# Stick-breaking attention in units of both heads of a pair, 128 queries and at most 512 keys

## The chip, the cores and the metric

One core of one Trainium2 chip runs the kernel. The metric is the device time of one launch in microseconds (us). A time is the median of several runs; one further execution was profiled, and every row of a trace is from it.

## The reference, cut to what matters

One layer of a decoder trunk on 1024 tokens of width 1024, all float32. A projection feeds three groups of heads: RWKV-7 (6 heads of 64), an RG-LRU, and stick-breaking attention (6 heads of 64). Then follow an output projection, a LayerNorm, a top-2 mixture of 16 experts and a second LayerNorm. The attention of one head, for each block of 128 queries (`i` = 0 to 7), is:

```python
kv_len = q0 + SBA_BLOCK
z = jnp.einsum('bhtd,bhsd->bhts', q[:, :, q0:kv_len], k[:, :, :kv_len]) * scale
mask = s_idx < t_idx
log_keep = jnp.where(mask, jax.nn.log_sigmoid(-z), 0.0)
after = lax.cumsum(log_keep, axis=3, reverse=True) - log_keep
attn = jnp.where(mask, jnp.exp(jax.nn.log_sigmoid(z) + after), 0.0)
outs.append(jnp.einsum('bhts,bhsd->bhtd', attn, v[:, :, :kv_len]))
```

The cumulative sum runs from the last key to the first, over at most 1024 keys.

## The kernel before

**Stages.** Every engine has its own program, and semaphores order them. The stages are: projection with the RG-LRU and the preparation of RWKV; the loop over 12 batches (the stage of the change, 373 to 900 us); output projection, first norm and router (900 to 1078 us); the mixture of experts (to about 1540 us); the last norm.

**The loop over batches.** A batch `b` is the RWKV delta rule on 256 tokens of one pair of heads: `mats_pe`, `mats_act`, `mats_dve` and `mats_pool`. It begins with products and masks (L646, L765), transposes (L656, L660), and then inverts triangular matrices in 5 levels. Each level is a chain over three engines: TensorE makes 16 small products (L602), ScalarE copies them out of PSUM (L742), TensorE makes 32 more, and VectorE writes them under a mask, first `lower`, then `upper` (L762). After the levels come L683, L689 to L707 and four state steps (L719, L726, L797), each of the last three with 4 bf16 matmuls of `keep_clock` (L629), which keep TensorE at work while it waits. After every fourth batch `rnorm_*` normalizes a pair's output.

**The attention between them.** The generators `mats_*` yield at 16 places (`GAPS`) in a batch. At each, `side_by_side` puts one piece of the attention into each engine's program: step `j` of `sba_pe`, `sba_act` and `sba_dve`. So the order on each engine is fixed when the kernel is built. A unit of the attention is one head, one block of 128 queries and all its keys (128 to 1024), 48 units in all, four steps each:

- kind 0: TensorE makes the scores z in `PS[0]` (L917, the head's 64 rows of the array; one matmul for each 512 keys) and adds the causal mask (L919, bf16). ScalarE makes Exp of the unit before (L951), and then Abs, Exp and Ln of this one (L965, L967, L969).
- kinds 1 and 2: TensorE transposes the unit before, up to four tiles in a step (L932), VectorE copies them out (L989). In kind 1 VectorE also takes max(z, 0) (L997), and in kind 2 it scans the keys backwards (L977) and subtracts (L979).
- kind 3: TensorE sums attention times v over all key tiles of the unit before (L940, the head's 64 columns of the array).

A float32 matmul stands in the trace as two records, a float32 transpose as one. The blocks of a pair are taken in the order 0, 7, 1, 6, 2, 5, 3, 4, so that four units (16 steps) always hold nine tiles for each head.

**The mixture of experts.** A loop of 21 rounds with two experts side by side on the column halves (L1499): gate, up, eight transposes of the next round's rows (L1493), four of the hidden values in two groups (L1529, L1534) whose copies VectorE and ScalarE make (L1589, L1564), and the down products. Ahead of the loop `keep_clock` runs 10 bf16 matmuls while the first rows are gathered.

Of the kernel before, what the change touches and what calls it, by code (L numbers as in the profile page):

```python
# [22 lines left out]
P = 128  # L23
# [3 lines left out]
HD = 64  # L27
# [27 lines left out]
def layer_kernel(nc, t, out):  # L55
    ctx = ExitStack()
    with ctx:
# [21 lines left out]
        pc = sb("pc", [P, NPAIR, S // C])  # L79

# [66 lines left out]
        s_bz, s_bx, s_bv = sem("z_in_psum"), sem("attn_transposed"), sem("attn_v_in_psum")  # L147
        s_bd, s_ba, s_bt, s_bo = sem("attn_dve"), sem("attn_act"), sem("attnT_copied"), sem("attn_out_copied")
# [668 lines left out]

# [66 lines left out]
        NU = NPAIR * NT * 2  # L884
        Rl = TT[:, 0, :]

        def unit(u):
            g, n, hh = u // (2 * NT), (u // 2) % NT, u % 2
            i = n // 2 if n % 2 == 0 else NT - 1 - n // 2
            return g, i, hh, slice(hh * HD, (hh + 1) * HD), (i + 1) * P, 1 + (i > 0)  # L890

        def group(i, k):

            cut = (i + 2) // 2
            return (0, cut) if k == 0 else (cut, i + 1)

        def groups(u):

            return sum(unit(x)[5] for x in range(u))
        BD, BA = 3, 4  # L900


        def sba_pe(e, j):
            u, kind = j // 4, j % 4
            if kind == 0:
                if u >= NU:
                    return
                g, i, hh, h, kv, ng = unit(u)
                wait(e, s_pe, LRU_T + SBA_T + NT)
                wait(e, s_bd, BD * u)  # L910
                for pair in range(1, NPAIR - 1):
                    if j == norm_step(pair) + 1:
                        wait(e, s_na, 2 * (pair - 1) + 1)
# [11 lines left out]
            g, i, hh, h, kv, ng = unit(u)  # L925
            if kind <= ng:
                k = kind - 1
                wait(e, s_ba, BA * u + 4)
                wait(e, s_bt, groups(u) + k)
                lo, hi = group(i, k)  # L930
# [882 lines left out]
```

## Time and profile before

| | |
|---|---|
| median of 3 runs | 1605.48 us (1601.74 to 1607.9) |
| the profiled execution's own time | 1605.52 us |
| its span, first to last instruction | 1603.8 us |
| outside the span | 1.7 us |
| TensorE busy | 1422.8 us (89%) |
| VectorE busy | 597.4 us (37%) |
| ScalarE busy | 431.4 us (27%) |
| mean granted TensorE clock | 0.944 of 2.4 GHz |

PE is TensorE's matmuls, PEld its weight loads, DVE VectorE, ACT ScalarE, POOL GpSimd. The granted clock of TensorE is either 1.0 (2.4 GHz) or 0.5 (1.2 GHz); a mean over a stretch lies between. The busy share of PE includes the tail of each matmul, so it is no measure of how full the array is.

### The profile page before, as it was taken

Reading aid. Unit: us, or ns where it says so; the run is one execution under the profiler, and the core shown is the slowest. Engines: PE = TensorE matmul, PEld = TensorE weight load, DVE = VectorE, ACT = ScalarE, POOL = GpSimd, SP = SyncE. Lnnn points to the kernel's source line nnn. Section 1 sums busy time; section 2 is a strip of 40 time slices with the busy share of each in tenths; the row PEclk is TensorE's granted clock in tenths of the full one; section 3 lists DMA queues with packets and bytes.
Section 4 is the critical chain, followed back from the end, with each engine's and each line's share of the span. In section 5 each row is a group of like instructions: output and inputs, shape, how many; then the busy total and the mean of one; then the engine's idle time right before and its main releaser. Section 6 shows DMA issues by size and latency. Waiting matters only on the chain.

```text
span 1603.8 us, 22792 instructions
## 1 busy us (share of the span) xinstructions
PE 1422.8 (89%) x9346; PEld 763.4 (48%) x9346; DVE 597.4 (37%) x1010; ACT 431.4 (27%) x671; POOL 102.7 (6%) x177
## 2 busy tenths in 40 slices
PE   8999999998888788887888999839999999999980
PEld 3444444455666566655666455514444444444430
DVE  2143103444667566656666333361011101111017
ACT  1044123322444334443434311121111111111113
POOL 0000000001000000000000000000110111111110
PEclk9999999999999988997999999859999999999995
DMA  4110111000000000002000225068749949959415
GB/s 185 38 40 31 35 39 40 27 0 1 1 2 2 1 1 2 1 2 106 1 2 2 81 92 210 27 238 299 271 137 352 338 128 320 340 168 317 117 32 217
DMA packets 61012, 170.14 MB, mean 106 GB/s; under 512 B 3184, under 2 KB 3328, under 8 KB 60928
## 3 DMA queue, kind: packets, MB, share of 16 engines
q1 hardware_dynamic: 54384, 145.31, 24.4%
q0 software_dynamic: 6544, 23.62, 6.1%
q8 instruction: 63, 1.03, 0.3%
q14 instruction: 21, 0.17, 0.0%
HBM read 144.28 MB, written 24.64 MB: 105 GB/s over the span
## 4 chain that ended last, share of the span: by engine, by line
PE 74%; DVE 15%; ACT 4%; issue 4%; DMA 2%; SPq 0%; DVEq 0%; POOL 0%; POOLq 0%; ACTq 0%
PE PS L1499 27%; PE PS L193 16%; PE PS L1123 7%; PE PS L602 4%; PE PS L917 3%; DVE TT L977 3%; PE PS L202 3%; DVE XS L762 2%; PE PS L940 2%; DVE XS L765 2%; PE PS L1493 1%; PE PS L932 1%; PE PS L336 1%; DMA YT<-x1d,RK 1%; PE PS L683 1%
## 5 line engine op out<-in xcount | busy, mean ns | idle before, releaser
L1499 PE MATMUL PS<-RK,YT 128*64 128x512 f32 x736 | 323.6, 596 | 0.8 <-DVE YT L1589 0.8
L193 PE MATMUL PS<-XS 128*128 128x512 f32 x672 | 294.6, 598 | 7.1 <-DMA XS<-in_xT 6.9
L1499 PE MATMUL PS<-XS,YT 128*64 128x512 f32 x656 | 287.3, 595 | 6.4 <-DVE YT L1589 5.5
L193 PEld LDWEIGHTS PS<-XS 128*128 128x128 f32 x672 | 127.3, 191 | 172.6 <-issue 164.2
L1499 PEld LDWEIGHTS PS<-XS,YT 128*64 128x64 f32 x656 | 89.0, 138 | 171.8 <-issue 170.7
L602 PE MATMUL PS<-XS 64*64 64x64 f32 x2688 | 110.9, 231 | 36.3 <-DVE XS L762 24.7
L602 PEld LDWEIGHTS PS<-XS 64*64 64x64 f32 x2688 | 95.1, 143 | 54.6 <-DVE XS L762 39.1
L1585 DVE TENSOR_TENSOR YT<-YT,PS 128x256 f32<-128x256 f32 x42 | 15.8, 419 | 271.8 <-PE PS L1499 271.8
L1123 PE MATMUL PS<-RK,YT 128*128 128x512 f32 x256 | 111.1, 593 | 1.1 <-DVE YT L1026 1.1
L1499 PEld LDWEIGHTS PS<-RK,YT 128*64 128x64 f32 x736 | 99.8, 137 | 20.7 <-issue 20.7
L1499 PE MATMUL PS<-SQ,YT 128*64 128x512 f32 x424 | 104.0, 593 | 1.9 <-DVE YT L1589 1.9
L1123 PEld LDWEIGHTS PS<-RK,YT 128*128 128x128 f32 x256 | 48.1, 190 | 59.8 <-issue 57.9
L762 DVE COPY_PREDICATED XS<-lower,PS 128x512 f32<-128x512 uint8 x60 | 43.5, 726 | 80.6 <-PE PS L602 69.7
L1598 DVE TENSOR_SCALAR YT<-PS,RK 128x512 f32<-128x512 f32 x21 | 15.8, 751 | 142.6 <-PE PS L1499 142.6
L977 DVE TENSOR_TENSOR_SCAN TT<-XS,TT 128x128 f32<-128x128 f32 (+7 forms) x48 | 66.0, 1374 | 1.0 <-ACT XS L969 0.5
L917 PE MATMUL PS<-SQ 64*128 64x512 f32 (+3 forms) x144 | 65.1, 562 | 0.6 <-ACT TT L1014 0.6
L742 ACT COPY XS<-PS 128x512 f32<-128x512 f32 x60 | 35.1, 584 | 109.2 <-PE PS L602 108.3
L1499 PEld LDWEIGHTS PS<-SQ,YT 128*64 128x64 f32 x424 | 38.0, 137 | 49.7 <-issue 49.7
L940 PE MATMUL PS<-XS,SQ 128*64 128x128 f32 x432 | 59.8, 285 | 0.0
L762 DVE COPY_PREDICATED XS<-upper,PS 128x512 f32<-128x512 uint8 x60 | 43.2, 720 | 36.0 <-PE PS L602 35.4
L1488 POOL DMA_INDIRECT sums<-YT,RK x21 | 33.6, 1600 | 328.9 <-DVE YT L1598 328.9
L1499 PE MATMUL PS<-YT 128*64 128x512 f32 x120 | 53.6, 593 | 0.0
(361 smaller groups left out, 1760.7 us busy)
## 6 DMA issues: line engine op xcount, KB each, us to landing
XS<-in_w_in SPq DMA_DIRECT2D x21, 512.0 KB, 3.2
XS<-in_w_gate SPq DMA_DIRECT2D x5, 2048.0 KB, 12.3
XS<-in_w_upx SPq DMA_DIRECT2D x5, 2048.0 KB, 18.0
XS<-in_w_down SPq DMA_DIRECT2D x5, 2048.0 KB, 9.1
RK<-in_w_gate SPq DMA_DIRECT2D x5, 2048.0 KB, 20.2
RK<-in_w_upx SPq DMA_DIRECT2D x5, 2048.0 KB, 22.6
RK<-in_w_down SPq DMA_DIRECT2D x5, 2048.0 KB, 13.1
SQ<-in_w_gate SPq DMA_DIRECT2D x4, 2048.0 KB, 21.3
```

Of the source, the lines that this page charges most:

```text
L193: m = e.matmul(acc[:, half * HB:(half + 1) * HB], XS[:, 8 + n % 4, kt * P:(kt + 1) * P], XS[:, kt, half * HB:(half + 1) * HB], start=kt == ...
L202: m = e.matmul(acc[:, 0:SBA_W], XS[:, kt, i * P:(i + 1) * P], wv[:, kt, :], start=kt == 0, stop=kt == KT - 1)
L602: ins = e.matmul(acc[r, m * P + d * C:m * P + (d + 1) * C], left[r, m, r], right[r, m, r], start=True, stop=True)
L742: e.copy(M1[:, :, :], four(RB(3))).then_inc(s_ma, 1)
L762: return e.copy_predicated(x[:, :, :], mask[:, lv:lv + 1, :].broadcast_to([P, 4, P]), src)
L765: e.tensor_tensor(AM[:, m, :, :], four(RB(m)), mask4[:, :, :], ALU.mult).then_inc(s_md, 1)
L917: ins = e.matmul(PS[0][:, lo:hi], SQ[h, g, i * P:(i + 1) * P], SQ[h, 3 + g, lo:hi], start=True, stop=not last)
L940: ins = e.matmul(PS[1][h, HB + (i % 4) * P:HB + (i % 4 + 1) * P], SV[:, st, g * P + hh * HD:g * P + (hh + 1) * HD], ATb[u % 2][:, st * P:( ...
L977: e.tensor_tensor_scan(R_[:, ::-1], E_[:, ::-1], R_[:, ::-1], 0.0, ALU.add, ALU.add).then_inc(s_bd, 1)
L1123: ins = e.matmul(PS[i % 2][:, half * HB:(half + 1) * HB], YT[:, kt, i * P:(i + 1) * P], WO[kt][:, half * HB:(half + 1) * HB], start=kt == ...
L1488: e.indirect_dma_start(sums, bass.IndirectOffsetOnAxis(put_tok, 0), Yb, None, compute_op=ALU.add)\
L1499: ins = e.matmul(acc[r, :], rows[:, r], third_cols(n, k, at, HB), start=start, stop=stop)
```

## The change

A unit becomes both heads of a pair, 128 queries and at most 512 keys, of which the later keys come first where a block has more than 512 (`SPANS`). There are 36 units. Each matmul of scores for head 0 is followed by that for head 1, which uses the other 64 rows of the array and another bank of PSUM. The sums with v alternate between the heads, that is between the column halves, and are split over two steps. VectorE's two scans of a unit (one for each head) take their start from `carry`, where the unit holds the rest of a longer block. ScalarE's operations, max, subtraction and copies hold both heads.

A unit has five steps (`KINDS`), a batch 15 places (`GAPS`): the last state step of a batch has no piece of the attention. On VectorE a scan that falls into the last three places of a batch is put behind the batch. In the mixture of experts half of the transposes of the next rows move behind those of the hidden values, and `keep_clock` ahead of the loop runs 16 matmuls for 10.

The diff, cut:

```diff
@@ -806,14 +808,14 @@
             for k, _ in enumerate(mats(e, b)):
-                if b + k:
+                if k < GAPS:
                     piece(e, batch_step(b) + k)
-        GAPS = 16
+        GAPS, KINDS = 15, 5
 
         def batch_step(b):
-            return GAPS * b + 4 * (b // NQ) - 1
+            return GAPS * b + 4 * (b // NQ)
...
+        SPANS = []
+        for n in range(NPAIR * NT):
+            i = n % NT // 2 if n % 2 == 0 else NT - 1 - n % NT // 2
+            kv = (i + 1) * P
+            cuts = [(HB, kv), (0, HB)] if kv > HB else [(0, kv)]
+            SPANS += [(n, n // NT, i, lo, hi, lo == cuts[0][0], lo == 0) for lo, hi in cuts]
+        NU = len(SPANS)
+        BD, BA = 4, 4
+        two = lambda x: x.rearrange("p (h c) -> p h c", h=2)
+        Z, R2 = two(PS[0][:, :]), two(Rl)
...
 (sba_pe, kind 0)
-                for lo in range(0, kv, HB):
-                    hi = min(kv, lo + HB)
-                    last = hi == kv
-                    ins = e.matmul(PS[0][:, lo:hi], SQ[h, g, i * P:(i + 1) * P], SQ[h, 3 + g, lo:hi],
-                                   start=True, stop=not last)
-                ins = e.matmul(PS[0][:, kv - P:kv], identb[:, :], causal_neg[:, :], start=False, stop=True)
+                w = hi - lo
+                for hh, h in heads:
+                    ins = e.matmul(Z[:, hh, 0:w], SQ[h, g, i * P:(i + 1) * P], SQ[h, 3 + g, lo:hi],
+                                   start=True, stop=not first)
+                if first:
+                    for hh, h in heads:
+                        ins = e.matmul(Z[:, hh, w - P:w], identb[:, :], causal_neg[:, :], start=False, stop=True)
...
 (sba_pe, kinds 1 and 2: head kind - 1; kinds 3 and 4)
+            cut = (len(tiles) + 1) // 2
...
+            for k in (range(cut) if kind == 3 else range(cut, len(tiles))):
+                for hh, h in heads:
                     ins = e.matmul(PS[1][h, HB + (i % 4) * P:HB + (i % 4 + 1) * P],
-                                   SV[:, st, g * P + hh * HD:g * P + (hh + 1) * HD],
-                                   ATb[u % 2][:, st * P:(st + 1) * P], start=st == 0, stop=st == i)
+                                   SV[:, tiles[k], g * P + hh * HD:g * P + (hh + 1) * HD],
+                                   AT2[u % 2][:, hh, k * P:(k + 1) * P], start=first and k == 0,
+                                   stop=last and k == len(tiles) - 1)
...
 (sba_scan)
+            for hh in range(2):
+                E_, R_ = E2[u % 2][:, hh, 0:w], R2[:, hh, 0:w]
+                e.tensor_tensor_scan(R_[:, ::-1], E_[:, ::-1], R_[:, ::-1], 0.0 if first else carry[:, hh:hh + 1],
+                                     ALU.add, ALU.add).then_inc(s_bd, 1)
+            wait(e, s_bd, BD * u + 3)
+            if not last:
+                e.tensor_copy(two(carry[:, :]), R2[:, :, 0:1]).then_inc(s_bc, 1)
+            e.tensor_tensor(E2[u % 2][:, :, 0:w], Z[:, :, 0:w], R2[:, :, 0:w], ALU.subtract).then_inc(s_bd, 1)
...
 (moe_pe)
-            keep_clock(e, PS[0][:, 0:HB], 10)
+            keep_clock(e, PS[0][:, 0:HB], 16)
...
                 e.wait_ge(s_xg, 16 * (i + 2))
-                xg_transposes(e)
+                xg_transposes(e, 0)
...
                 ins.then_inc(s_htp2, 1)
+                xg_transposes(e, 1)
...
 (the program of VectorE)
-                u = (batch_step(b) + GAPS - 1) // 4
-                side_by_side(mats_dve, lambda e, j: sba_dve(e, j, j < 4 * u), e, b)
-                if u < NU:
-                    sba_scan(e, u)
+                late = [j for j in range(batch_step(b) + GAPS - 3, batch_step(b) + GAPS) if j % KINDS == 2]
+                side_by_side(mats_dve, lambda e, j: sba_dve(e, j, j not in late), e, b)
+                for j in late:
+                    if j // KINDS < NU:
+                        sba_scan(e, j // KINDS)
```

## Rows read from the trace of the kernel before

**Rows 1.** The page: busy time by engine, and the granted clock in 40 slices

```profile
PE 1422.8 (89%) x9346; PEld 763.4 (48%) x9346; DVE 597.4 (37%) x1010; ACT 431.4 (27%) x671; POOL 102.7 (6%) x177
...
PEclk9999999999999988997999999859999999999995
```

**Rows 2.** Three stretches, each one batch (the second with a norm behind it)

```profile
core 0: us, PE busy (x) PEld busy (x) DVE busy (x) ACT busy (x) POOL busy (x), PEclk, DMA share, GB/s
...
449.00:489.00 40.00, 34.85 (x483) 26.39 (x479) 26.50 (x46) 16.42 (x32) 3.81 (x4) 0.96 0.01 2
...
669.00:725.00 56.00, 43.78 (x502) 30.23 (x500) 33.45 (x56) 22.85 (x43) 2.35 (x4) 0.91 0.01 2
725.00:772.00 47.00, 41.11 (x472) 30.15 (x473) 26.84 (x45) 17.16 (x32) 2.35 (x4) 0.78 0.24 91
```

**Rows 3.** Chain that ended last, 373 to 889 us, shares by line

```profile
by line: PE PS L602 11.3%; PE PS L917 10.7%; DVE TT L977 9.5%; issue 8.2%; DVE XS L762 6.0%; PE PS L940 5.8%; DVE XS L765 4.9%; PE PS L932 4.4%; PE PS L683 3.2%; PE PS L629 2.5%; DVE XS L979 2.4%; DVE TT L997 2.3%; PE PS L719 2.1%; DVE XS L
```

**Rows 4.** Scores and sums with v: all records, ns min/median/max, first and last start, forms

```profile
L917 PE MATMUL PS<-SQ x144: 269/589/1217, 378.8 to 870.9; 64*128 64x512 f32 x72, 64*128 64x128 f32 x24, 64*128 64x256 f32 x24, 64*128 64x384 f32 x24
...
L940 PE MATMUL PS<-XS,SQ x432: 272/273/476, 389.8 to 886.4; 128*64 128x128 f32 x144
```

**Rows 5.** Groups of the page: busy us, mean ns of one

```profile
L917 PE MATMUL PS<-SQ 64*128 64x512 f32 (+3 forms) x144 | 65.1, 562 | 0.6 <-ACT TT L1014 0.6
L940 PE MATMUL PS<-XS,SQ 128*64 128x128 f32 x432 | 59.8, 285 | 0.0
```

**Rows 6.** Timeline of weight loads at 709 us: start, us; one 128x512 record follows each

```profile
709.47 0.19 PEld L336 LDWEIGHTS PS<-RK,head_ones 128*128 128x128 f32 x1 [0.24 <-issue]
709.90 0.19 PEld L336 LDWEIGHTS PS<-RK,head_ones 128*128 128x128 f32 x1 [0.24 <-issue]
```

**Rows 7.** Timeline of PE: matmuls on halves (L700 to L701 16 records)

```profile
660.37 0.45 PE L700 MATMUL PS<-XS 128*64 128x128 f32 x4
...
661.07 0.44 PE L701 MATMUL PS<-XS 128*64 128x128 f32 x4
...
662.13 1.52 PE L940 MATMUL PS<-XS,SQ 128*64 128x128 f32 x12
...
668.58 2.27 PE L646 MATMUL PS<-RK 64*128 64x256 f32 x16
...
732.23 1.98 PE L917 MATMUL PS<-SQ 64*128 64x512 f32 x4
...
743.13 3.78 PE L917 MATMUL PS<-SQ 64*128 64x512 f32 x4
```

**Rows 8.** Timeline: two levels of a batch, one of them held by VectorE's scan

```profile
642.41 0.68 PE L602 MATMUL PS<-XS 64*64 64x64 f32 x16 [0.38 <-DVE XS L762]
643.02 1.55 PE L917 MATMUL PS<-SQ 64*128 64x512 f32 x4
643.14 0.59 ACT L742 COPY XS<-PS 128x512 f32<-128x512 f32 x1 [3.19 <-PE PS L602]
...
644.51 0.23 PE L919 MATMUL PS<-causal_neg,identb 128*128 128x128 bf16 x1
644.67 1.15 PE L602 MATMUL PS<-XS 64*64 64x64 f32 x32
...
645.46 0.73 DVE L762 COPY_PREDICATED XS<-lower,PS 128x512 f32<-128x512 uint8 x1 [2.51 <-PE PS L602]
...
646.25 0.68 PE L602 MATMUL PS<-XS 64*64 64x64 f32 x16
```

**Rows 9.** VectorE's groups of the attention by form: busy us, mean ns of one

```profile
L977 DVE TENSOR_TENSOR_SCAN TT<-XS,TT 128x1024 f32<-128x1024 f32 x6 | 14.1, 2358 | 0.7 <-ACT XS L969 0.5
L977 DVE TENSOR_TENSOR_SCAN TT<-XS,TT 128x512 f32<-128x512 f32 x6 | 7.4, 1234 | 0.0
L979 DVE TENSOR_TENSOR XS<-PS,TT 128x1024 f32<-128x1024 f32 x6 | 7.3, 1224 | 0.2
L979 DVE TENSOR_TENSOR XS<-PS,TT 128x512 f32<-128x512 f32 x6 | 4.2, 692 | 0.2
L989 DVE COPY XS<-PS 128x512 f32<-128x512 f32 x18 | 12.4, 689 | 6.4 <-PE PS L932 6.4
L965 ACT ACTIVATE XS<-PS 128x1024 f32<-128x1024 f32 x6 | 6.1, 1024 | 9.6 <-PE PS L919 9.6
L965 ACT ACTIVATE XS<-PS 128x512 f32<-128x512 f32 x6 | 3.6, 594 | 2.9 <-PE PS L919 2.9
```

**Rows 10.** Timeline behind the second pair's norm: the attention's operations

```profile
724.84 0.42 DVE L977 TENSOR_TENSOR_SCAN TT<-XS,TT 128x128 f32<-128x128 f32 x1
...
725.29 0.29 DVE L979 TENSOR_TENSOR XS<-PS,TT 128x128 f32<-128x128 f32 x1
```

**Rows 11.** Stretches before and behind a fall of the clock; 373 to 900 us

```profile
735.20:738.50 3.30, 1.47 (x36) 1.10 (x32) 3.20 (x5) 2.82 (x4) 0.00 (x0) 1.00 0.44 171
738.50:752.20 13.70, 12.19 (x112) 7.99 (x109) 7.40 (x8) 5.42 (x7) 0.00 (x0) 0.50 0.00 1
...
373.00:900.00 527.00, 445.38 (x5689) 323.45 (x5688) 327.96 (x549) 213.93 (x402) 31.31 (x48) 0.92 0.03 10
```

**Rows 12.** Timeline of a round of the experts, from the last up product to the first down product

```profile
1117.65 0.59 PE L1499 MATMUL PS<-RK,YT 128*64 128x512 f32 x1
1118.17 1.10 PE L1493 MATMUL PS<-ident,YT 128*128 128x128 f32 x8
1118.28 0.75 DVE L1585 TENSOR_TENSOR YT<-YT,PS 128x256 f32<-128x256 f32 x2 [12.80 <-PE PS L1499]
1119.11 0.38 PE L1529 MATMUL PS<-ident,YT 128*128 128x128 f32 x2
1119.33 0.38 PE L1534 MATMUL PS<-ident,YT 128*128 128x128 f32 x2
1119.53 0.43 DVE L1589 COPY YT<-PS 128x256 f32<-128x256 f32 x1 [0.49 <-PE PS L1529]
...
1120.10 0.61 PE L1499 MATMUL PS<-XS,YT 128*64 128x512 f32 x1 [0.39 <-DVE YT L1589]
```

**Rows 13.** The start of the experts' loop: timeline, then a stretch

```profile
1072.56 4.26 PE L629 MATMUL PS<-restart,identb 128*128 128x512 bf16 x10
...
1077.99 1.09 PE L1493 MATMUL PS<-ident,YT 128*128 128x128 f32 x8 [1.17 <-DMA YT<-x1d,RK]
...
1078.90:1082.30 3.40, 2.49 (x8) 0.86 (x8) 0.69 (x1) 1.87 (x2) 1.35 (x3) 0.65 1.04 388
```

More of the change, by code:

```diff
@@ L878, in rnorm_dve @@
             sba_dve(e, norm_step(g) + 3)
-        NU = NPAIR * NT * 2
         Rl = TT[:, 0, :]
[L887 to L900, printed above, removed]
+        SPANS = []
[8 more added lines that the diff above has]
+        Z, R2 = two(PS[0][:, :]), two(Rl)
+        E2, AT2 = [two(x) for x in Eb], [two(x) for x in ATb]
+        carried = [sum(not x[6] for x in SPANS[:u]) for u in range(NU + 1)]
+        heads = [(hh, slice(hh * HD, (hh + 1) * HD)) for hh in range(2)]
+        z_issued, z_after_norm = [0], [0]
         def sba_pe(e, j):
-            u, kind = j // 4, j % 4
+            u, kind = j // KINDS, j % KINDS
             if kind == 0:
@@ L907, in sba_pe @@
                     return
[L908 removed]
+                n, g, i, lo, hi, first, last = SPANS[u]
                 wait(e, s_pe, LRU_T + SBA_T + NT)
                 wait(e, s_bd, BD * u)
[L911 to L919 removed]
+                wait(e, s_na, z_after_norm[0])
+                z_issued[0] = u + 1
+                w = hi - lo
[5 more added lines that the diff above has]
+                        ins = e.matmul(Z[:, hh, w - P:w], identb[:, :], causal_neg[:, :], start=False, stop=True)
                 ins.then_inc(s_bz, 1)
@@ L924, in sba_pe @@
                 return
-            g, i, hh, h, kv, ng = unit(u)
-            if kind <= ng:
-                k = kind - 1
+            n, g, i, lo, hi, first, last = SPANS[u]
+            tiles = range(lo // P, hi // P)
+            if kind <= 2:
+                hh = kind - 1
                 wait(e, s_ba, BA * u + 4)
-                wait(e, s_bt, groups(u) + k)
-                lo, hi = group(i, k)
-                for st in range(lo, hi):
-                    ins = e.transpose(PS[1][:, (st - lo) * P:(st - lo + 1) * P], Eb[u % 2][:, st * P:(st + 1) * P],
-                                      ident[:, :])
+                wait(e, s_bt, 2 * u + hh)
+                for k in range(len(tiles)):
+                    ins = e.transpose(PS[1][:, k * P:(k + 1) * P], E2[u % 2][:, hh, k * P:(k + 1) * P], ident[:, :])
@@ L934, in sba_pe @@
                 ins.then_inc(s_bx, 1)
+                return
+            cut = (len(tiles) + 1) // 2
             if kind == 3:
-                wait(e, s_bt, groups(u + 1))
-                if hh == 0:
-                    wait(e, s_bo, u // 2)
-                for st in range(i + 1):
+                wait(e, s_bt, 2 * u + 2)
+                if first:
+                    wait(e, s_bo, n)
+            ins = None
+            for k in (range(cut) if kind == 3 else range(cut, len(tiles))):
+                for hh, h in heads:
@@ L1020, in snorm_pe @@
             wait(e, s_ns, g + 1)
-            wait(e, s_bd, BD * min((norm_step(g + 1) + 1) // 4, NU))
+            wait(e, s_bd, BD * z_issued[0])
+            z_after_norm[0] = 2 * g + 1 if sums is PS[0] else z_after_norm[0]
             heads_sum(e, sums, x).then_inc(s_np, 1)
@@ L1489, in moe_pool, with xg_transposes @@
                  .then_inc(s_ys, 16)
-        def xg_transposes(e):
-            for kt in range(KT):
+        def xg_transposes(e, half):
+            for kt in range(half * KT // 2, (half + 1) * KT // 2):
                 ins = e.transpose(PS[1][:, kt * P:(kt + 1) * P], Xg[:, kt * P:(kt + 1) * P], ident[:, :])
-            ins.then_inc(s_xgp, 1)
+            if half == 1:
+                ins.then_inc(s_xgp, 1)
         def two_experts(e, acc, rows, n, at, start, stop):
@@ L1503, in moe_pe @@
             ahead(e, s_xgp, s_htp, s_htp2, s_y1)
-            keep_clock(e, PS[0][:, 0:HB], 10)
+            keep_clock(e, PS[0][:, 0:HB], 16)
             e.wait_ge(s_xg, 16)
-            xg_transposes(e)
+            for half in range(2):
+                xg_transposes(e, half)
             e.wait_ge(s_tab, 1)
```

47 lines of the change are left out of this document (24 added, 23 removed).

## The prediction, as put on record before the changed kernel ran

> **What bounds the kernel now.** I read the page first. TensorE is busy 89% of the span, VectorE 37%, and the row of the granted clock shows 8s and 9s in the middle [rows 1]. The reader is to see that TensorE is the engine to relieve, but that an average says nothing of the stage that is edited. So I read the stretches. A batch takes 40 to 47 us (56 where a norm follows), with PE busy 35 to 41 us and VectorE about 27 us of it. Where the clock is 0.96 a batch takes 40 us, at 0.78 it takes 47 [rows 2]. Third, the chain of waits from 373 to 889 us (516 us). No engine holds it alone: scores (L917) have 10.7%, 55.2 us, sums with v (L940) 5.8%, 29.9 us, VectorE's scans, subtractions and maxima (L977, L979, L997) 14.2%, 73 us, "issue" 8.2%, and the rest is mostly the chain of levels [rows 3]. Fourth, one level in the timeline: TensorE's 16 products at 642.41, the copy at 643.14, 32 products at 644.67, the mask write at 645.46, the next level at 646.25, so 3.84 us. Without a wait for the score piece it would be about 3.0: the copy ended at 643.73, and the 32 products could start only after 1.55 us of scores and the causal mask, at 644.67 [rows 8]. A piece of the attention is free as far as it fits into TensorE's pauses of a level, roughly 0.8 us each, and what is longer delays both recurrences.
>
> **Scores on both row halves.** Removed is half of the array time. A 128x512 record takes 0.43 us at full clock [rows 6], 0.84 ns a column. The 144 records have 72x512 + 24x(128 + 256 + 384) = 55,296 columns [rows 4], 46.4 us, which with tails, switches and half clock became 65.1 us busy [rows 5]. Do row halves run together? The 16 records of L646, 64 rows each, alternate between the halves in fours: 2.27 us over 16 is at most 0.142 us a record of 256 columns, where one after the other they need 0.215 [rows 6, 7]. So yes. The new order changes halves every two records and has nothing else between, so I take one half.
>
> **Sums on both column halves.** L940 keeps to one half: 12 records in 1.52 us, one alone 0.27 [rows 4], (1.52 - 0.27)/11 = 0.114 us each. L700 and L701 have the same size and alternate: their 16 records last from 660.37 to 661.07 + 0.44, (1.14 - 0.27)/15 = 0.058 us each [rows 7]. Again one half, and here both halves write the same bank in the trace too. Of 432 records, 49 us, about 24 go.
>
> **What of it reaches the end.** The two lines are on the chain for 85.1 of 124.9 us busy [rows 3, 5], 68%. Half of the 85.1 is 42.5 us, the upper bound. But where TensorE's piece gets shorter, the level next waits for VectorE. I take two thirds, **-28 us**; the lower bound is one third, -14, if VectorE's 73 us of the chain take over where they are close behind. The pieces are also evener. The longest score piece had four 512-column records (3.78 us at half clock, 1.98 at full, [rows 7]), now 1.05 us of record pairs; the sums had up to 16 records at 0.114, 1.8 us, and have now 8 at 0.058, 0.5 us, which fits into a pause. There are 12 units fewer, each with about 0.2 us of change between 64-row and 128-row matmuls (two records of 512 and two of 256 need 1.29 us, and from 643.02 to the mask's 644.51 it is 1.49, [rows 8]): **-2 us**, between 0 and -4.
>
> **VectorE and ScalarE.** The elements are the same. A scan of 1024 becomes two of 512: 2 x 1.234 against 2.358, +0.1 us [rows 9]. The fixed part of a VectorE operation is about 0.16 us (two of 512 at 0.692 against one of 1024 at 1.224). So 24 more scans and 12 carries are +5.8, 12 maxima, 12 subtractions and 18 copies fewer are -6.7: **0**. ScalarE has 48 operations fewer at 2 x 0.594 - 1.024 = 0.16 us fixed, -8 us, and none of it counts while it is busy 17 of 40 us [rows 2]. The new waits (the scan for the carry of the unit before) are for VectorE's own work of several steps ago: 0. What queues behind a scan is the mask write of the next level. The block in kind 2 is 0.69 + 2.47 + 0.15 + 1.22 = 4.5 us for the widest unit, as before (4.3), but 18 of 36 units are this wide where 12 of 48 had over 768 keys. Excess over what a unit's steps can hide (two levels before, two and a half now, each with 1.56 us of VectorE free beside its 1.44 of mask writes) sums to 17.6 us a pair before and 17.2 after, by 0.6 + 5.7 us per 1024 columns. So 0, with -5 to +10.
>
> **The place behind a norm.** The units shift against the batches. After the second pair's eighth batch the four steps in the norm used to hold a block of 128 keys, and now one of 1024: three ScalarE operations of 1.0 us, and a scan block of 3.7 for 0.7 us, ahead of the next batch's masks [rows 9, 10]. **+4 us**, between 0 and 6. The dropped place in the last state step is nothing.
>
> **The clock.** Rows show what precedes a fall: in 735.2 to 738.5 PE was busy 1.5 of 3.3 us while VectorE was busy all along, at full clock, and then it ran at 0.50 for 13.7 us [rows 11]. With 60 us less of PE in the stage, more stretches look like that. The price, from the batches: 47 us at 0.78 and 40 at 0.96 [rows 2] is 39 us for each 1.0 of clock and batch, over 12 batches 4.7 us for each 0.01 of the stage's mean, which is now 0.92 [rows 11]. I count on 0.90: **+9 us**, between 0 and +40. The Trainium skill, "TensorE: Matmul & The Clock Gate", section "Why this matters for your kernels", warns of long idle gaps only; every wait in this stretch is shorter, so by it this term would be 0 and the sum nine lower. The trace disagrees with the page, and I go by the trace.
>
> **The experts.** In a round TensorE's last up product starts at 1117.65, eight transposes run from 1118.17, and the hidden ones come at 1119.11 and 1119.33, though VectorE's first product was done at about 1118.66. The down products then wait 0.39 us for the copy, until 1120.10 [rows 12]. With four transposes moved behind, the hidden ones start near 1118.8, the copies near 1119.2, and the four moved lie over the copies: the down products start when the 12 transposes are through, about 1119.8. That is 0.3 us, 21 times: **-6 us**, between 0 and -8. The copies of the next rows come 0.9 us later and have the down products to hide in. The six more bf16 matmuls (0.43 us each at half clock) run from 1076.8 to 1079.4 or, at full clock, to 1078.1; the rows were there at 1077.99 [rows 13]. They may spare the stretch at 0.65 behind: 1.2 us of its 3.4. **-1 us**, between +1.4 and -1.2.
>
> **Sum.** -28 - 2 + 0 + 4 + 9 - 6 - 1 = -24 us. The profiled execution took 1605.5 (1603.8 span and 1.7 around it), and the median of the runs is the same, so 1581.5, and I say 1581 us.
>
> **Rivals.**
> - *Clock takes it back* (the other side). The stage's mean falls to 0.84: +37 for +9, 1609 us; at 0.83 or under it is slower by over 0.5%. For it: the falls come where VectorE holds the chain, and that time stays while PE's shrinks. Against: `keep_clock` stands in the state steps, and a stretch at half clock fills PE up again. From 0.86 down it costs the gain. Chance 0.2.
> - *TensorE's pieces are wholly on the path*, and the clock holds: -42.5 - 4 - 7 = -53, 1552 us. For it: the "issue" share. Chance 0.15.
> - *VectorE becomes the bound*: only the third of 42.5 comes through, -14 for -28, 1595 us. For it: 14.2% of the chain [rows 3], and VectorE busy throughout the 3.3 us before the fall [rows 11]. The Trainium skill's "TensorEngine Tiling (Array Packing)", section "PSUM Bottleneck", says this in general: tiling speeds TensorE and not what empties PSUM. Chance 0.15.
> - *The halves don't run together*, since the sums write one bank: only the experts and evener pieces, about 1599 us. L700 and L701 speak against it [rows 7]. Chance 0.05.
> - The forecast, 1581 us (1565 to 1595 by itself), has 0.45.
>
> **Range and chances.** No change that a measurement can tell is within 0.5%, 8 us: 1597.5 to 1613.5. Faster: the forecast's 0.45, 0.15, most of the 0.15 and a little of the others, 0.71. Slower: a mean clock under 0.83, 0.09. Same: 0.20. The range from 1553 to 1609 leaves out the better half of the second case and the worse half of the first.
>
> **What would show it.** Scores in pairs of records with starts almost together, L917 busy near 35 us and L940 near 30; batches of 37 to 38 us where the clock is 0.96; a stage clock of 0.90; the down products of a round 0.3 us earlier. Wrong it would be by a stage clock under 0.86, by waits of TensorE for L762 that grow by more than 15 us, or by records of two halves that start a full record apart.

## The result, and the profile after

The changed kernel takes 1628.78 us, the median of 4 runs (1626.51 to 1630.46), where the kernel before took 1605.99 beside it. The ratio is 1.0151, with a 95% interval from 1.0129 to 1.0173: it is slower by 1.5%. Forecast were 1581 us, and a range that ended at 1609.

TensorE is busy 26 us less, and the span is 25 us longer. The page, TensorE's busy time and the granted clock in 40 slices, to be read beside [rows 1]:

```profile
PE 1396.9 (86%) x9352; PEld 713.6 (44%) x9352; DVE 597.7 (37%) x1004; ACT 422.5 (26%) x623; POOL 99.5 (6%) x177
...
PEclk9999999999889788879999899959999999999995
```

The stage of the batches as one stretch, from its first matmul (L646, now L648) to the first of the output projection, in the kernel before and in the changed one. Then two batches of the changed one (the second with the first norm behind it). The columns are those of [rows 2]:

```profile
372.97:900.40 527.43, 445.44 (x5690) 323.52 (x5689) 328.26 (x549) 214.32 (x402) 31.31 (x48) 0.92 0.03 10
```

```profile
372.72:930.90 558.18, 416.96 (x5689) 300.43 (x5688) 326.61 (x543) 203.39 (x354) 28.10 (x48) 0.88 0.03 9
411.00:454.40 43.40, 34.34 (x472) 25.15 (x470) 25.66 (x44) 15.39 (x28) 2.35 (x4) 0.84 0.01 2
497.50:563.50 66.00, 43.32 (x508) 28.47 (x506) 37.78 (x59) 20.68 (x35) 2.35 (x4) 0.86 0.00 1
```

Before, the stage was 527.4 us with 445.4 of TensorE's time in it, so TensorE stood still for 82.0 us. Now it is 558.2 with 417.0, and it stands still for 141.2 us. TensorE's busy time fell by 28.5 us, its idle time rose by 59.2, and the stage is 30.8 us longer for it. What lies behind the stage got shorter by 5.6 us (703.4 from its end to the end of the span, now 697.8), which leaves the 25 us of the span.

The work itself did what the change says. The two groups of the attention's matmuls, by line over the whole span, against 65.1 and 59.8 us in [rows 5]:

```profile
L944 PE MATMUL PS<-XS,SQ 128*64 128x128 f32 x432 | 42.0, 311 | 2.9 <-DVE XS L1002 2.7
L916 PE MATMUL PS<-SQ 64*128 64x512 f32 (+3 forms) x144 | 40.9, 651 | 3.0 <-DVE XS L993 1.7 <-ACT TT L1027 1.3
```

So the question is what TensorE waits for. First the view of waits of the kernel before, TensorE's, 373 to 900 us (in total, times, longest), then the same of the changed kernel, 372 to 930 us:

```profile
PE PS L602 <- DVE XS L762: 24.7, 28, 2.4
...
PE PS L602 <- ACT XS L742: 10.6, 18, 1.7
PE PS L656 <- DVE XS L765: 9.0, 7, 2.5
...
PE PS L683 <- DVE XS L762: 3.2, 6, 0.6
```

```profile
PE PS L604 <- ACT XS L744: 39.7, 35, 3.0
PE PS L604 <- DVE XS L764: 26.0, 19, 2.5
PE PS L658 <- DVE XS L767: 16.5, 10, 2.7
PE PS L685 <- DVE XS L764: 16.0, 7, 3.3
PE PS L648 <- DVE YT L879: 12.2, 2, 6.4
PE PS L691 <- ACT XS L748: 6.9, 4, 2.5
```

L604 is L602 of before, L744 is L742, L764 is L762, L767 is L765, L658 is L656 and L685 is L683. Half of the new idle time, 29.1 us, is spent waiting for ScalarE's copy of a level (L744). Two more have VectorE behind them: the matmuls behind the last level (L685), +12.8 us, and the transposes at the head of a batch (L658), which wait for its masks, +7.5 us. The mask writes between levels, the wait that the prediction watched, are nearly unchanged (+1.3).

One such wait in the timeline of the changed kernel (third pair, second level; start, us, engine and line):

```profile
669.99 1.15 PE L604 MATMUL PS<-XS 64*64 64x64 f32 x32 [0.41 <-ACT XS L744]
...
671.07 1.13 PE L916 MATMUL PS<-SQ 64*128 64x512 f32 x4
...
672.12 0.68 PE L604 MATMUL PS<-XS 64*64 64x64 f32 x16
...
672.24 1.02 ACT L972 ACTIVATE XS<-PS 128x1024 f32<-128x1024 f32 x1 [1.72 <-PE PS L916]
...
673.30 1.06 ACT L974 ACTIVATE XS<-XS 128x1024 f32<-128x1024 f32 x1
...
674.38 1.06 ACT L976 ACTIVATE XS<-XS 128x1024 f32<-128x1024 f32 x1
675.35 0.57 ACT L744 COPY XS<-PS 128x512 f32<-128x512 f32 x1
...
676.06 1.15 PE L604 MATMUL PS<-XS 64*64 64x64 f32 x32 [2.88 <-ACT XS L744]
```

The 16 products that the copy waits for are done at 672.80. Without the score piece ScalarE would be free for it, but in its program the three operations of the scores (Abs, Exp, Ln) come first. They could start only with the scores, at 672.24, and so the copy comes at 675.35, and TensorE stands still for 2.88 us. The score piece stood behind the 32 products of level 1. Before, the pieces of kind 0 fell on the places 1, 5, 9 and 13 of a batch, the first three of them always behind the 16 products of a level (the odd places up to 9), where the level's copy is ahead of Abs on ScalarE and the 32 products give the three operations cover [rows 8]. With 15 places and five steps they fall on 0, 5, 10 in the first pair, on 1, 6, 11 in the second and on 2, 7, 12 in the third: in each batch one of three is behind the last products of a level (10, 6 or 2).

The waits stand where this puts them. Of the 35 waits for the copy in the changed kernel eight are over 2.5 us, one in each batch of the second and the third pair (2.60 to 2.99 us, 22.5 us in sum). In the first pair place 10 is behind the last level, so no copy of a level follows. There it is the copy behind L685 (L748) that comes late, 6.9 us of waits where L746, its name before, had 3.3.

### The profile page after: what moved, and what is told of

It is laid out like the page before. It is cut to its first block, busy times and chain, and to the rows that moved or that the text cites. A ratio compares the mean times of both kernels' runs of the same rounds, so it can differ in the third digit from the quotient of the medians.

```text
span 1628.7 us, 22664 instructions
## 1 busy us (share of the span) xinstructions
PE 1396.9 (86%) x9352; PEld 713.6 (44%) x9352; DVE 597.7 (37%) x1004; ACT 422.5 (26%) x623; POOL 99.5 (6%) x177
## 4 chain that ended last, share of the span: by engine, by line
PE 72%; DVE 14%; ACT 6%; issue 4%; DMA 2%; SPq 0%; DVEq 0%; POOL 0%; POOLq 0%; ACTq 0%
PE PS L1514 26%; PE PS L195 16%; PE PS L1137 7%; PE PS L604 4%; DVE TT L988 4%; PE PS L204 3%; PE PS L916 2%; DVE XS L764 2%; PE PS L1507 1%; DVE XS L767 1%; PE PS L933 1%; PE PS L631 1%; PE PS L338 1%; DMA YT<-x1d,RK 1%; PE PS L944 1%
## 5 line engine op out<-in xcount | busy, mean ns | idle before, releaser
L604 PE MATMUL PS<-XS 64*64 64x64 f32 x2688 | 115.6, 237 | 66.3 <-ACT XS L744 39.7
L604 PEld LDWEIGHTS PS<-XS 64*64 64x64 f32 x2688 | 99.9, 148 | 93.6 <-issue 52.7
L1137 PE MATMUL PS<-RK,YT 128*128 128x512 f32 x256 | 111.1, 593 | 1.1 <-DVE YT L1040 1.1
L1137 PEld LDWEIGHTS PS<-RK,YT 128*128 128x128 f32 x256 | 48.1, 190 | 59.8 <-issue 57.9
L764 DVE COPY_PREDICATED XS<-lower,PS 128x512 f32<-128x512 uint8 x60 | 43.6, 726 | 76.5 <-PE PS L604 63.9
L744 ACT COPY XS<-PS 128x512 f32<-128x512 f32 x60 | 34.8, 580 | 109.3 <-PE PS L604 109.0
L1002 DVE COPY XS<-PS 128x512 f32<-128x512 f32 (+3 forms) x72 | 39.8, 553 | 55.8 <-PE PS L933 55.5
L1514 PEld LDWEIGHTS PS<-SQ,YT 128*64 128x64 f32 x424 | 33.0, 137 | 52.4 <-issue 52.4
L933 PE MATMUL PS<-ident,XS 128*128 128x128 f32 x216 | 42.6, 310 | 9.0 <-DVE XS L1002 5.6
L1587 ACT ACTIVATE YT<-PS,RK 128x512 f32<-128x512 f32 x21 | 14.4, 687 | 138.2 <-PE PS L1514 138.2
L226 DVE SCALAR_TENSOR_TENSOR RK<-PS,vec,RK 128x1023 f32<-128x1023 f32 x11 | 14.1, 1284 | 97.6 <-ACT RK L215 97.6
## 6 DMA issues: line engine op xcount, KB each, us to landing
RK<-in_w_down SPq DMA_DIRECT2D x5, 2048.0 KB, 12.8
```

The lines of the kernel that those rows point to most:

```text
L604: ins = e.matmul(acc[r, m * P + d * C:m * P + (d + 1) * C], left[r, m, r], right[r, m, r], start=True, stop=True)
L744: e.copy(M1[:, :, :], four(RB(3))).then_inc(s_ma, 1)
L764: return e.copy_predicated(x[:, :, :], mask[:, lv:lv + 1, :].broadcast_to([P, 4, P]), src)
L933: ins = e.transpose(PS[1][:, k * P:(k + 1) * P], E2[u % 2][:, hh, k * P:(k + 1) * P], ident[:, :])
L1002: e.tensor_copy(AT2[v % 2][:, hh, 0:w], PS[1][:, 0:w]).then_inc(s_bt, 1)
L1137: ins = e.matmul(PS[i % 2][:, half * HB:(half + 1) * HB], YT[:, kt, i * P:(i + 1) * P], WO[kt][:, half * HB:(half + 1) * HB], start=kt == ...
```

## The experiments

Each is compared with the kernel before on the same chip: medians 1605.12 us (17 runs) for the first four, 1606.15 (13 runs) for the next four, and 1605.24 to 1607.16 for the rest. These medians differ by up to 2 us from chip to chip, and so may two experiments that ran on different chips.

**e1_aligned**: the changed kernel with its work kept and its places moved. Four steps a unit (all sums in one), twelve pieces a batch, no scan put off.

```diff
             for k, _ in enumerate(mats(e, b)):
-                if k < GAPS:
-                    piece(e, batch_step(b) + k)
+                if 1 <= k <= GAPS:
+                    piece(e, batch_step(b) + k - 1)
-        GAPS, KINDS = 15, 5
+        GAPS, KINDS = 12, 4
-            cut = (len(tiles) + 1) // 2
+            cut = len(tiles)
...
-                late = [j for j in range(batch_step(b) + GAPS - 3, batch_step(b) + GAPS) if j % KINDS == 2]
+                late = []
```

> The changed kernel with its 36 units in four steps each (all sums with v in the fourth) and 12 places in a batch, the ones behind the first product of a level first: a score piece always comes behind a level's 16 products, never behind its 32, as in the kernel before. No scan is put off. Phase theory (five steps against levels of two places put the score piece, and with it ScalarE's four operations, in front of a level's copy): ScalarE's copies of a level wait about 6 us in sum in place of 31, and the time is 1570 to 1590. Width theory (a unit of 1024 columns holds ScalarE and VectorE wherever it stands): 1610 to 1630. Clock theory (less work of TensorE alone lets the clock fall): the mean stays at 0.93 or under and the time over 1610.

Measured: 1574.6 us, ratio 0.9826 [0.9805, 0.9847], faster than both kernels. Its stage as a stretch, and its waits of TensorE:

```profile
372.05:871.70 499.65, 388.51 (x5689) 281.92 (x5688) 327.17 (x543) 202.96 (x354) 28.12 (x48) 0.92 0.03 10
```

```profile
PE PS L604 <- DVE XS L764: 46.7, 38, 3.2
PE PS L604 <- ACT XS L744: 14.4, 19, 1.2
```

The same work on the same halves, 54 us faster than the changed kernel. The waits for the copy are back to short ones (14.4 us in sum, more than the 6 I expected); TensorE now waits mostly for VectorE's mask writes. The stage's 58.5 us are not waits alone: TensorE stands still for 111.1 us instead of 141.2, and the same number of records keeps it busy for 388.5 us instead of 417.0, at a mean clock of 0.92 instead of 0.88.

**e2_before_shifted**: the kernel before, with all its pieces one place later (2, 6, 10 and 14 for the scores); not one operation is changed.

```diff
-                if b + k:
-                    piece(e, batch_step(b) + k)
+                piece(e, batch_step(b) + k)
-            return GAPS * b + 4 * (b // NQ) - 1
+            return GAPS * b + 4 * (b // NQ)
...
-                    if j == norm_step(pair) + 1:
+                    if j == norm_step(pair):
```

> The kernel before with every piece of the attention one place later, so that a score piece comes behind a level's 32 products; nothing else changes, units and widths are the old ones. Phase theory: slower by 15 to 40 us than the kernel before (1620 to 1645), with the copies of a level waiting over 20 us. Width theory and clock theory: within 8 us of the kernel before.

Measured: 1653.77 us, ratio 1.0315 [1.029, 1.034]. The shift alone costs 49 us, more than the 15 to 40 expected. Its stage, and its longest row of waits, which was 10.6 us in the kernel before:

```profile
373.16:944.40 571.24, 459.95 (x5690) 339.56 (x5689) 329.25 (x549) 212.33 (x402) 29.06 (x48) 0.89 0.02 9
```

```profile
PE PS L602 <- ACT XS L742: 63.1, 41, 3.0
```

Here too both terms grow: TensorE's idle time from 82.0 to 111.3 us, and its busy time from 445.4 to 460.0 with not one record more, while the mean clock falls from 0.92 to 0.89.

**e3_experts_only**: the kernel before with the two edits of the experts' part, nothing of the attention.

```diff
-            keep_clock(e, PS[0][:, 0:HB], 10)
+            keep_clock(e, PS[0][:, 0:HB], 16)
-                xg_transposes(e)
+                xg_transposes(e, 0)
...
                 ins.then_inc(s_htp2, 1)
+                xg_transposes(e, 1)
```

> The kernel before with the edits of the experts alone (half of the transposes moved, 16 matmuls of keep_clock). By the rows of the changed kernel, from the first output projection to the end it takes 697.8 us for 703.4: 5 to 7 us faster than the kernel before. If that was the stage's start or chance: within 2 us.

Measured: 1601.48 us, ratio 0.9971 [0.9956, 0.9985], 2 to 7 us saved by the interval.

**e4_before_half**: the kernel before, in its own order, with part of the computation left out: 2432 of each head's 4608 columns of scores are made, and the sums go over the later 20 of 36 tiles of keys. It prices TensorE's time in these pieces without moving any.

```diff
+                    lo = (lo + hi) // 2 if not last else min((lo + hi) // 2, hi - P)
-                for st in range(i + 1):
+                for st in range((i + 1) // 2, i + 1):
```

> The kernel before with about half of the array work of the attention left out: scores only for 2432 of 4608 columns of a head, sums only over the later 20 of 36 tiles. ScalarE and VectorE do all their work. It prices TensorE's time in the old order of pieces. If the prediction's two thirds were right: 25 to 30 us faster, 1576 to 1580. If VectorE's and ScalarE's work is right behind: 0 to 12 us faster. If less work lets the clock fall by more than it saves: slower.

Measured: 1579.61 us, ratio 0.9856 [0.9836, 0.9876]. Scores are busy 40.6 us for 65.1 and sums 38.3 for 59.8: of 46 us taken out, 20 to 26 came through. With all this work gone and the order kept, the mean clock of the stage is still 0.91:

```profile
373.22:872.30 499.08, 405.43 (x5497) 307.19 (x5496) 329.29 (x549) 213.37 (x402) 31.32 (x48) 0.91 0.03 10
```

**e8_aligned_later**: e1_aligned with everything one place later.

```diff
-                if 1 <= k <= GAPS:
-                    piece(e, batch_step(b) + k - 1)
+                if 2 <= k <= GAPS + 1:
+                    piece(e, batch_step(b) + k - 2)
```

> The aligned kernel (four steps, 12 places, 1574.6 us) with every piece one place later: a score piece behind a level's 32 products in place of its 16. Units, widths and the number of pieces are the same. Phase theory: as the kernel before lost 49 us by the same shift, 1600 to 1625 here, with copies of a level waiting over 30 us in sum for 16.5. If the four steps or the free places gave the gain and not the phase: within 8 us of 1574.6.

Measured: 1630.95 us, ratio 1.0155 [1.0127, 1.0183]. One place is worth 56 us here, and it brings e1_aligned to where the changed kernel is (the range expected ended at 1625; the 16.5 us that it gives for e1_aligned's waits for the copy are 14.4 in the view above). Stage and waits for the copy:

```profile
372.75:930.10 557.35, 415.44 (x5690) 303.19 (x5689) 330.32 (x543) 206.44 (x354) 28.18 (x48) 0.88 0.03 9
```

```profile
PE PS L604 <- ACT XS L744: 60.8, 40, 3.0
```

**e7_scalar_split**: the changed kernel, with ScalarE's Exp and Ln of a unit in kind 1, one place after its Abs. TensorE's and VectorE's programs keep their order.

```diff
                 e.activation(E_, Z[:, :, 0:w], ACT.Abs).then_inc(s_ba, 1)
+            if kind == 1 and u < NU:
+                w = SPANS[u][4] - SPANS[u][3]
+                E_ = E2[u % 2][:, :, 0:w]
                 e.wait_ge(s_ba, BA * u + 1)
                 e.activation(E_, E_, ACT.Exp, scale=-1.0).then_inc(s_ba, 1)
```

> The changed kernel (1628.8 us) with ScalarE's Exp and Ln of a unit one place behind its Abs, so that the copy of a level can come between. If ScalarE's three operations in front of the copy are what the phase costs: the copies' waits fall from 31.6 to under 15 us and the time to 1600 to 1615. If it is TensorE's score piece itself in front of the level's 16 products, or the clock: 1622 to 1635.

Measured: 1602.11 us, ratio 0.9969 [0.9952, 0.9985], 27 us under the changed kernel with no work removed. The waits of TensorE:

```profile
PE PS L604 <- DVE XS L764: 28.8, 27, 2.5
PE PS L685 <- DVE XS L764: 18.7, 8, 3.3
PE PS L604 <- ACT XS L744: 16.9, 33, 1.2
PE PS L658 <- DVE XS L767: 16.6, 10, 2.7
```

The longest wait for the copy fell from 3.0 to 1.2 us, and the sum from 39.7 to 16.9. (The 31.6 us that two of the expectations give for the changed kernel is too low; the view above has 39.7.) The waits behind VectorE stayed or grew.

**e6_filled**: the changed kernel, with two bf16 matmuls of 256 columns (`keep_clock`) ahead of TensorE's waits in levels 2 to 5, to hold the clock and leave the order alone.

```diff
             for lv in range(1, LEVELS):
+                if lv > 1:
+                    keep_clock(e, RB(1)[:, 0:256], 2)
                 wait(e, s_tl, b * NTL + lv)
...
                 yield
+                if lv > 1:
+                    keep_clock(e, RB(1)[:, 0:256], 2)
                 wait(e, s_ul, b * NUL + lv)
```

> The changed kernel with two 256-column bf16 matmuls of keep_clock ahead of each product of levels 2 to 5 (16 more calls of two a batch at most, on a bank that is free there). Clock theory: the stretches at half clock fall from 136 us to under 90, and the time to 1605 to 1620, though the fillers take up to 0.4 us each where TensorE isn't waiting. If the clock only follows the waits and costs little: 1630 to 1645.

Measured: 1623.99 us, ratio 1.0101 [1.0072, 1.0131]. A miss: it lies between the two ranges. The clock rose as meant, and the time fell by only 5 us. Its stage, and then the group of `keep_clock` (L631) in the changed kernel and in this one:

```profile
372.62:927.00 554.38, 429.52 (x5881) 304.38 (x5880) 326.06 (x543) 203.48 (x354) 28.11 (x48) 0.91 0.03 9
```

```profile
L631 PE MATMUL PS<-restart,identb 128*128 128x256 bf16 x144 | 22.7, 282 | 0.0
```

```profile
L631 PE MATMUL PS<-restart,identb 128*128 128x256 bf16 x336 | 60.5, 280 | 0.0
```

The fillers are themselves 37.8 us of TensorE's busy time. Without them it is busy for 391.7 us, where the changed kernel has 417.0, and it stands still for 124.9 us instead of 141.2. So the run doesn't price the clock: what the higher clock and the shorter waits gave back, the fillers took again.

**e5_no_late**: the changed kernel, each scan at its own place.

```diff
-                late = [j for j in range(batch_step(b) + GAPS - 3, batch_step(b) + GAPS) if j % KINDS == 2]
+                late = []
```

> The changed kernel without putting scans off behind a batch: a scan that falls into the state steps runs there. In the changed kernel 12 scans of 1024 columns stand between a batch and the next one's masks or the norm (3.7 us each). If that order costs: 1605 to 1620, and the batch with the first norm takes under 60 us for 66. If the state steps lose as much by a scan among them: 1625 to 1640.

Measured: 1637.92 us, ratio 1.0203 [1.0164, 1.0241]. A miss: at its place 12, 13 or 14 the third scan of a batch holds up the state steps instead. The 9 us to the changed kernel are not sure, since the two intervals overlap. TensorE's waits in the stage have a new row, and that for L767 is gone from the longest ten:

```profile
PE PS L721 <- DVE XS L799: 19.6, 10, 2.6
```

**e12_scores_early**: the changed kernel with its five steps and put-off scans, but a score piece that falls on place 2, 6 or 10 goes one place earlier, behind 16 products; 12 of 36 pieces move.

```diff
-                if k < GAPS:
+                if k < GAPS and not scores_early(b, k):
                     piece(e, batch_step(b) + k)
+                if scores_early(b, k + 1):
+                    piece(e, batch_step(b) + k + 1)
+        def scores_early(b, k):
+            return k in (2, 4, 6, 8, 10) and (batch_step(b) + k) % KINDS == 0
```

> The changed kernel, still five steps in 15 places and scans put off, but each score piece (with ScalarE's operations of kind 0) that falls behind the 32 products of a level goes one place earlier, behind the 16 products: 12 of 36 pieces. Theory of places: these pieces cost most of what separates the changed kernel from e1_aligned (54 us), so 1600 to 1614 us, waits of TensorE for the level's copy 8 to 15 us for 31.6. Rival (five steps for four, with the scans put off behind a batch, hold the time, wherever the scores stand): 1622 to 1632 us.

Measured: 1611.12 us, ratio 1.0033 [1.0017, 1.0049], 18 us under the changed kernel by twelve moved pieces. The waits for the copy fell to 20.2 us, less far than the 8 to 15 expected.

**e13_early_split**: e12_scores_early with the split of e7_scalar_split.

> As e12_scores_early, and ScalarE's Exp and Ln one place later than its Abs. If place and order are the same cause, the two edits don't add: within 8 us of the better of e7_scalar_split (1602 us) and e12_scores_early. If ScalarE's row of three costs time also where the scores stand behind 16 products (the start of a batch, the norms), they add in part: 1585 to 1594 us.

Measured: 1605.1 us, ratio 0.9994 [0.9978, 1.0009], as good as e7_scalar_split and no better. The two edits don't add, which is what the expectation gives where both remove one cause. The waits for the copy are down to 9.9 us, and those for VectorE stand:

```profile
PE PS L604 <- DVE XS L764: 34.7, 37, 2.5
PE PS L685 <- DVE XS L764: 22.3, 12, 3.3
PE PS L658 <- DVE XS L767: 16.6, 10, 2.7
```

**e14_aligned_put_off**: e1_aligned, but the scan at place 11, behind the levels, is put off behind the batch.

```diff
-                late = []
+                late = [batch_step(b) + 10]
```

> The kernel e1_aligned, with the one scan of each batch that stands behind the levels (place 11) put off behind the batch, as the changed kernel does it with its third unit. Theory: the put-off scan stands ahead of VectorE's masks of the next batch, TensorE waits for them before L658 (16.6 us in e13_early_split, none in e1_aligned), and this is the larger part of the 28 us that lie between them: 1588 to 1602 us. Rival (behind the batch a scan is as well off as at place 11, and the 28 us belong to five steps, with their last scan ahead of level 5): 1570 to 1580 us.

Measured: 1596.51 us, ratio 0.9941 [0.992, 0.9962], 22 us over e1_aligned for one moved scan a batch. VectorE's timeline at the end of a batch, first in e14_aligned_put_off, then the same batch in e1_aligned:

```profile
485.10 0.41 DVE L804 TENSOR_TENSOR RK<-PS,XS 128x256 f32<-128x256 f32 x1
485.43 2.45 DVE L987 TENSOR_TENSOR_SCAN TT<-XS,carry,TT 128x512 f32<-128x512 f32 x2
487.92 1.22 DVE L992 TENSOR_TENSOR XS<-PS,TT 128x1024 f32<-128x1024 f32 x1
489.06 2.47 DVE L767 TENSOR_TENSOR XS<-PS,mask 128x512 f32<-128x512 f32 x4
```

```profile
473.04 2.69 DVE L987 TENSOR_TENSOR_SCAN TT<-XS,carry,TT 128x512 f32<-128x512 f32 x2
475.76 1.22 DVE L992 TENSOR_TENSOR XS<-PS,TT 128x1024 f32<-128x1024 f32 x1
...
481.42 0.41 DVE L804 TENSOR_TENSOR RK<-PS,XS 128x256 f32<-128x256 f32 x1
482.44 2.48 DVE L767 TENSOR_TENSOR XS<-PS,mask 128x512 f32<-128x512 f32 x4 [0.61 <-PE PS L648]
```

Put off, scan and subtraction are 3.7 us ahead of the next batch's masks, which come 3.96 us after L804; with the scan at place 11 they come 1.02 us after it. TensorE's waits for the masks in e14_aligned_put_off:

```profile
PE PS L658 <- DVE XS L767: 16.2, 9, 2.7
```

**e9_aligned_split**: e1_aligned with the split of e7_scalar_split.

> The kernel e1_aligned with ScalarE's Exp and Ln of a unit one place later than its Abs. Theory of places: in e1_aligned every score piece already stands beside 16 products of a level, ScalarE has the level's copy ahead of the Abs in most of them, and the split has little left to give: 1568 to 1577 us against 1574.6, waits of TensorE for the level's copy 8 to 16 us. Rival (ScalarE's three operations in a row cost the same wherever the piece stands): the 27 us that the split gave in the changed kernel come again, about 1550 us.

Measured: 1576.6 us, ratio 0.9813 [0.9785, 0.984]. Nothing left to give: the split helps only where Abs, Exp and Ln stand ahead of a copy that TensorE waits for.

**e10_aligned_filled**: e1_aligned with the fillers of e6_filled.

> The kernel e1_aligned with keep_clock (two bf16 matmuls of 256 columns) ahead of the waits of levels 2 to 5. Theory of places: the clock follows the waits, so that fillers give the stage's mean 0.01 to 0.03 and the time little, 1568 to 1580 us, as in e6_filled. Rival (the lower clock holds time of its own also here): a mean of 0.95 or more in the stage and 10 us or more saved, under 1565 us.

Measured: 1583.02 us, ratio 0.9842 [0.9811, 0.9873], no gain, and the median rather worse, 3 us over the range expected. Here the fillers take 40.8 us of TensorE's busy time (the group of L631 is 62.8 us for 22.0), and the stage's mean clock is 0.93 for 0.92.

## Why the prediction was wrong

The sign was wrong, and the step that failed is the one that put VectorE and ScalarE at **0**, and with it the claim that ScalarE's saved operations and the new order cost nothing. In its place the runs show some 50 us that hang on the order: one place later costs the kernel before 49 us, and the work of the change in another order is 54 us faster. I counted what each engine has to do, and not where in its fixed program it does it. "None of it counts while it is busy 17 of 40 us" is an average: ScalarE was idle before and behind the piece, and was busy in just the 3 us in which TensorE waited for its copy. The diff had it all: 16 places and four steps for 15 and five. I worked out where the units shift behind a norm and not where the kinds of a step shift against the levels.

Step by step:

- **Scores and sums on halves, the array time**: right. Four records of 512 columns on the two row halves last 1.13 us, where four on one half lasted 1.98 [rows 7]. The groups fell to 40.9 and 42.0 us busy, not to the 35 and 30 of the forecast, so that less array time went than its half. In e1_aligned, with the clock at 0.92, they are 38.6 and 31.8.
- **Two thirds of 42.5, -28 us**: right in size. e4_before_half took 46 us busy out, which by the same shares (68% on the chain, two thirds of it) is 21 us, and measured 20 to 26. And e1_aligned, with this work and the experts' edits, is 31 us under the kernel before (this one is no clean test, since it also has no put-off scan, where the kernel before has one in each batch).
- **VectorE and ScalarE, 0 (-5 to +10)**: this failed. ScalarE's part: e7_scalar_split and e13_early_split, which take it away in two ways, gain 24 to 27 us. e12_scores_early gains 18 by the place of twelve pieces. And e2_before_shifted shows a cost of the same kind, 49 us, in the kernel before, with three of the four score pieces of a batch behind 32 products (places 2, 6 and 10).
- **The put-off scan**: part of the same term. It was a 0 too, and rightly against the kernel before in so far as that also puts scans off. But the third unit of each batch is always both heads with 512 keys (1024 elements, 3.7 us), where the kernel before puts off one head's unit: TensorE's waits for the masks rose from 9.0 to 16.5 us. In the kernel of four steps the place of this scan is worth 22 us (e14_aligned_put_off to e1_aligned). In the changed kernel leaving it in place gains nothing, as e5_no_late shows (+9 us).
- **The place behind a norm, +4 (0 to 6)**: the place that it names came out near this, the batch with the second norm grew by 4.9 us (56.6 to 61.5). The batch with the first norm wasn't counted, and it grew by 12.7 us (53.3 to 66.0). That is no cause of its own: with ScalarE's split the first is 58.3, in e1_aligned 55.6, and in e14_aligned_put_off, where only the scan is put off, 62.2.
- **The clock, 0.90, +9**: too small, and with the wrong cause. The mean came to 0.88, which by the price of 4.7 us for 0.01 is 19 us. I expected the fall because TensorE has less to do. But e4_before_half takes 46 us of TensorE's work out and keeps 0.91 (0.92 before), and e1_aligned has all the saved work and 0.92. The order moved it: 0.92 to 0.89 in e2_before_shifted, and from e1_aligned's 0.92 to 0.88 in e8_aligned_later and to 0.89 in e14_aligned_put_off. What in the order moves it is not shown: e1_aligned and e2_before_shifted both stand still for 111 us, at 0.92 and 0.89. The price was no overcharge: e8_aligned_later is busy for 26.9 us more than e1_aligned (415.4 for 388.5) with the same work and order of steps, and the rest of the 57.7 us between the two stages is idle time. Busy time includes the tails of matmuls, so not all of the 26.9 need be the clock. How the 54 us divide between waits and clock is shown by no run, since in e6_filled the fillers took 37.8 us themselves. The Trainium skill, "TensorE: Matmul & The Clock Gate", section "Why this matters for your kernels", warns of long idle gaps only. By it the clock would have held in e2_before_shifted. The trace disagrees: no wait there was over 3.0 us but the two behind the norms, up to 6.1 us (6.5 before), and the mean still fell from 0.92 to 0.89.
- **The experts, -6, and the start, -1**: right in sign. From the last up product to the first down product it takes 2.25 us (below) for 2.45 [rows 12], 21 times 0.2 us, 4 us for 6. e3_experts_only measured 2 to 7.

The round of the experts in the changed kernel, timeline of TensorE and VectorE:

```profile
1146.31 0.59 PE L1514 MATMUL PS<-RK,YT 128*64 128x512 f32 x1
...
1146.83 0.66 PE L1507 MATMUL PS<-ident,YT 128*128 128x128 f32 x4
...
1147.42 0.44 PE L1545 MATMUL PS<-ident,YT 128*128 128x128 f32 x2
...
1148.03 0.60 PE L1507 MATMUL PS<-ident,YT 128*128 128x128 f32 x4
...
1148.56 0.64 PE L1514 MATMUL PS<-XS,YT 128*64 128x512 f32 x1
```

The wait for the copy is gone: the first down product has none.

Of the rivals, "Clock takes it back" had the right side and neither the mean (0.84) nor the time (1609 us, 20 under what was measured); the lower clock is there, but it came with the order. "VectorE becomes the bound" fits e1_aligned, whose longest row is 46.7 us of waits for the mask writes (24.7 before), but no run took VectorE's work away to show it, and it doesn't make the changed kernel slow. My list of what would show the forecast wrong had the wrong wait in it: it watched VectorE's masks between the levels (+1.3 us), and not ScalarE's copy (+29.1 us).

The account from the changed kernel to the best of the runs, 1628.8 to 1574.6, each term with its share of the clock: 24 us by ScalarE's order (to 1605.1, e13_early_split), 22 us by the put-off scan (measured in the kernel of four steps), and 8 us left. For these 8 the waits of L685 are the candidate, 22.3 us in e13_early_split and 3.7 in e1_aligned, since with five steps a scan often stands ahead of the last level's mask write. No run took it alone, so it stays open. That the terms add is assumed, not measured.

## What to carry to other kernels

Where pieces of one computation are woven into the fixed programs of in-order engines, the place of a piece against the recurrence is a cost of its own. Before a change of the number of steps or places, write out which piece falls on which place, and for each engine what then stands ahead of the operation that another engine waits for. Put a piece where the second engine already has its part of the recurrence ahead of it in its program and isn't needed for a while behind it (here: the score piece behind the 16 products, with the level's copy ahead of Abs). Shift the whole pattern by one place as an experiment: it costs a few lines, and here it was worth 49 and 56 us, more than the whole gain that the change was made for. A busy share of 40% says nothing of the 3 us in which the engine is needed.

## What the runs showed of the hardware

- Two float32 matmuls on the two row halves run together also when one matmul (two records) on one half is followed by one on the other: 1.13 us for four records of 512 columns, for 1.98 before. Twelve records of sums on alternating column halves lasted 0.88 us in e1_aligned, where twelve on one half lasted 1.52 [rows 7], and both halves wrote the same bank of PSUM.
- The granted clock fell without a long gap. In e2_before_shifted, with not one operation changed, the mean of the stage fell from 0.92 to 0.89, and no wait but the two behind the norms was over 3.0 us. The batch of the changed kernel from 411.0 to 454.4 us had TensorE busy 34.34 of 43.40 us and a mean of 0.84.
- Fillers on TensorE can hold the clock and still give little. Those that raised the stage's mean from 0.88 to 0.91 took 37.8 us of TensorE's time and gave 5 us back (e6_filled). In e10_aligned_filled, with the pieces in better places, 40.8 us of them gave nothing (1583.0 us, where the split kernel beside it took 1576.6).
